# Nine buffers for x, loaded ahead of the tables, and half of the first channel tile's products between the last transposes, in a decoder trunk step

## What is computed

```
xn = rmsnorm(x, norm1_g)
proj = xn @ w_in                 # 1024 -> 2816 columns
conv_out = conv_mixer(proj[..., :1024])      # GLU, causal depthwise conv of width 31, LayerNorm, swish
rwkv_out = rwkv_mixer(proj[..., 1024:])      # RWKV-7 time mixing, 8 heads of 64
h = x + concat(conv_out, rwkv_out) @ w_out
h = h + hier_moe(rmsnorm(h, norm2_g))        # top group of 4, then top 2 of its 8 experts
y = rmsnorm(h, norm_f_g)
```

## Time and profile before

| | |
|---|---|
| median of 3 runs | 1312.06 us (1311.66 to 1314.58) |
| the profiled execution, its own time | 1316.22 us |
| its span | 1314.5 us |
| TensorE busy | 1156.6 us (88%) |
| VectorE, ScalarE, GpSimd busy | 706.1, 326.5, 224.3 us |
| chain that ended last, by engine | TensorE 78%, VectorE 11%, DMA 4% |

### The profile page before, as it was taken

How to read it: one execution, slowest core, us unless ns; L and a number is a source line. 1 busy time by engine, 2 the same in 40 slices (tenths; PEclk the granted TensorE clock), 3 DMA queues, 4 the chain that set the end, 5 groups by cost and what they waited for, 6 DMA issues and landing times.

```text
span 1314.5 us, 23739 instructions
## 1 busy us (share of the span) xinstructions
PE 1156.6 (88%) x9144; PEld 662.7 (50%) x9145; DVE 706.1 (54%) x1252; ACT 326.5 (25%) x616; POOL 224.3 (17%) x278
## 2 busy tenths in 40 slices
PE   4999999999999599999979899984599999999910
PEld 3455555555545588888866455553233333333300
DVE  4278889972224578888852223227243344344346
ACT  4100001111202245555531112111122232322221
POOL 5000000000002212333300001000232333333000
PEclk9799999999998799999987999985699999999965
DMA  6411111110000110111232221127479989999556
GB/s 206 101 32 32 33 32 35 38 38 20 0 0 1 15 17 15 18 19 17 40 87 105 87 74 64 40 83 327 168 282 335 328 317 336 397 408 409 226 220 225
DMA packets 100794, 171.81 MB, mean 131 GB/s; under 512 B 47751, under 2 KB 72190, under 8 KB 91423
## 3 DMA queue, kind: packets, MB, share of 16 engines
q1 hardware_dynamic: 93215, 152.70, 32.9%
q0 software_dynamic: 7488, 17.84, 3.8%
HBM read 153.83 MB, written 26.11 MB: 137 GB/s over the span
## 4 chain that ended last, share of the span: by engine, by line
PE 78%; DVE 11%; DMA 4%; issue 3%; ACT 2%; SPq 1%; POOL 0%; ACTq 0%; POOLq 0%; DVEq 0%
PE ps L1417 26%; PE ps L1847 14%; PE ps L1721 10%; PE ps L1877 7%; PE ps L1444 4%; PE ps L1465 2%; PE ps L1834 2%; DMA arena<-y_rows 2%; DVE arena L2151 1%; PE ps L1749 1%; PE ps L1453 1%; DMA arena<-in_x_prompt_dram 1%; DVE arena L2154 1%; PE ps L1431 1%; PE ps L1661 1%
## 5 line engine op out<-in xcount | busy, mean ns | idle before, releaser
L1417 PE MATMUL ps<-arena 128*128 128x512 f32 (+1 forms) x1056 | 347.6, 491 | 0.6 <-ACT arena L898 0.6
L1417 PEld LDWEIGHTS ps<-arena 128*128 128x128 f32 x1056 | 175.8, 192 | 173.6 <-issue 172.9
L1847 PE MATMUL ps<-arena 128*64 x416 | 192.6, 607 | 7.0 <-DVE arena L2545 6.0
L1850 PE MATMUL ps<-arena 128*64 128x512 f32 x416 | 192.6, 607 | 0.0
L1977 DVE SCALAR_TENSOR_TENSOR arena<-arena,cw 128x1024 f32<-128x1024 f32 x240 | 168.2, 780 | 0.4
L1721 PE MATMUL ps<-arena 128*128 128x512 f32 (+1 forms) x288 | 128.3, 600 | 0.0
L1847 PEld LDWEIGHTS ps<-arena 128*64 128x64 f32 x416 | 55.7, 139 | 118.4 <-issue 118.4
L1444 PE MATMUL ps<-arena 64*64 64x64 f32 x2864 | 98.8, 222 | 13.8 <-DVE arena L2163 9.9
L1444 PEld LDWEIGHTS ps<-arena 64*64 64x64 f32 x2864 | 92.1, 138 | 18.8 <-DVE arena L2163 11.0
L1877 PE MATMUL ps<-arena 128*64 x208 | 96.5, 607 | 2.4 <-ACT arena L1230 2.4
L1880 PE MATMUL ps<-arena 128*64 128x512 f32 x208 | 96.5, 607 | 0.0
(11 more groups left out here) (323 smaller groups left out, 1527.1 us busy)
## 6 DMA issues: line engine op xcount, KB each, us to landing
arena<-in_w_exp_gate_dram SPq DMA_DIRECT2D x32, 1024.0 KB
arena<-in_w_exp_up_dram SPq DMA_DIRECT2D x32, 1024.0 KB
arena<-in_w_exp_down_dram SPq DMA_DIRECT2D x32, 1024.0 KB, 8.7
arena<-in_w_in_dram SPq DMA_DIRECT2D x22, 512.0 KB, 4.0
arena<-in_x_prompt_dram SPq DMA_DIRECT2D x16, 512.0 KB, 6.0
arena<-y_rows SPq DMA_DIRECT2D x8, 1024.0 KB
arena<-in_w_out_dram SPq DMA_DIRECT2D x2, 2048.0 KB, 9.5
xn_rows<-arena SPq DMA_DIRECT2D x8, 512.0 KB, 2.9
```

The source lines that it names most:

```text
L1417: ins = pe.matmul(pr[:, n0:n1], win[q % 6][:, c, :], xnT[:, c, n0:n1], start=(c == 0), stop=(c == DC - 1))
L1847: pe.matmul(banks(b)[0:HS, :], xgT[b][:, c, 0:HS], wring_gu[:, bass.ds(slot, 1), 0:2, c, :].rearrange("p a w f -> p (a w) f"), start=(c == ...
L1850: ins = pe.matmul(banks(b)[HS:P, :], xgT[b][:, c, HS:P], wgu[b][:, :, c, :], start=(c == 0), stop=(c == DC - 1))
```

## The change

`x_in` gets nine places, in the part of the arena that later holds zs, so no load of x waits for a buffer. SyncE issues x0, the gain, x1, x2, x3, the first w_in tile, x4 to x7, the second w_in tile, x8, then the 18 tables, then w_in tiles 2 to 5. Nine semaphores (`x_here`) tell of the tiles; six of them are used later for other ends, whose counts therefore start at 16 (`16 + ...` in those waits). The transposes of x use PSUM banks 4 to 7 instead of 0 to 3. The eight products of the first 512 tokens of q = 0 (blocks c = 0 to 7) are laid behind the transposes of tiles 5, 6, 7 and 8, two each. The tables' transposes come behind them all, into banks 3, 6 and 7, and VectorE unloads them after its last copy. The wait for the unloaded tables stands before q = 1. ScalarE runs one Sqrt on a column of zeros first, which loads its table ahead of the first square.

```diff
-        x_in = [at(O_XR + s * D, D) for s in range(3)]
+        x_in = [at(O_ZS + (1 + s) * D, D) for s in range(NT)]
...
+        x_here = [*x_loaded, s_loaded, fin_stored, *xn2_stored]
...
+        x_here += fin_out
...
             def load_x(i):
-                if i >= 3:
-                    sp.wait_ge(xn_done, i - 2)
                 src = x_prompt[0, i * P:(i + 1) * P, :] if i < NT - 1 else x_sample.rearrange("b t d -> (b t) d")
-                sp.dma_start(x_in[i % 3][0:rows_of(i), :], src).then_inc(x_loaded[i % 3], 16)
+                sp.dma_start(x_in[i][0:rows_of(i), :], src).then_inc(x_here[i], 16)
...
             load_x(0)
             sp.dma_start(gain[:, :], norm1_g[0, :].partition_broadcast(P)).then_inc(gain1_in, 16)
-            load_x(1)
-            load_x(2)
+            for i in range(1, NT):
+                load_x(i)
+                if i in (3, 7):
+                    load_w_in(i // 7)
...
-            for i in range(3, NT):
-                load_x(i)
...
+            act.wait_ge(iota_done, 1)
+            act.activation(stat[:, 7, 0:1], stat[:, 7, 0:1], ACT.Sqrt)
             square(0)
...
             def tables():
                 pe.wait_ge(tables_in, 16 * N_TABLES)
-                tb = banks(6)
+                pe.wait_ge(xT_act, NT - 1)
+                pe.wait_ge(xT_dve, NT - 1)
+                tb = banks(3)
...
                 for c in range(DC):
-                    ins = pe.transpose(banks(2 * (i % 2) + c // 4)[:, (c % 4) * P:(c % 4) * P + r],
+                    ins = pe.transpose(banks(4 + 2 * (i % 2) + c // 4)[:, (c % 4) * P:(c % 4) * P + r],
                                        xn[i % 2][0:r, c * P:(c + 1) * P], ident[0:r, 0:r])
                 ins.then_inc(xT_psum, 1)
-                if i == 3:
-                    tables()
-
+                if i == 5:
+                    pe.wait_ge(w_loaded[0], 16)
+                if i >= 5:
+                    for c in range(2 * i - 10, 2 * i - 8):
+                        pe.matmul(banks(0), win[0][:, c, :], xnT[:, c, 0:512], start=(c == 0), stop=(c == DC - 1))
+            tables()
             pe.wait_ge(xT_act, NT)
             pe.wait_ge(xT_dve, NT)
-            pe.wait_ge(tables_done, 1)
-            pe.wait_ge(const_ready, 2)
...
             for q in range(MT):
                 pe.wait_ge(w_loaded[q % 6], 16 * (q // 6 + 1))
+                if q == 1:
+                    pe.wait_ge(tables_done, 1)
+                    pe.wait_ge(const_ready, 2)
...
-                for n0 in range(0, N, 512):
+                for n0 in range(0 if q else 512, N, 512):
...
-                if i == 5:
+                if i == NT - 1:
+                    copy_T(i)
                     dve.wait_ge(tables_psum, 1)
-                    tb = banks(6)
+                    tb = banks(3)
```

More of the change, by code:

```diff
@@ L434, in hybrid_decoder_step @@
         wd_in = [w_loaded[5], *x_loaded]
-        wd_0 = [16 * len(range(5, MT, 6))] + [32 * (NT // 3)] * 3
+        wd_0 = [16 * len(range(5, MT, 6))] + [16 + 16 * (NT // 3)] * 3
         gu_here, wd_here, gu_copied, down_copied = (sem(n) for n in ("gu_here", "wd_here", "gu_copied", "down_copied"))
@@ L466, in load_x, with load_w_in @@
             def load_x(i):
-                if i >= 3:
-                    sp.wait_ge(xn_done, i - 2)
                 src = x_prompt[0, i * P:(i + 1) * P, :] if i < NT - 1 else x_sample.rearrange("b t d -> (b t) d")
-                sp.dma_start(x_in[i % 3][0:rows_of(i), :], src).then_inc(x_loaded[i % 3], 16)
+                sp.dma_start(x_in[i][0:rows_of(i), :], src).then_inc(x_here[i], 16)
+            def load_w_in(q):
+                t = ORDER[q]
+                sp.dma_start(win[q % 6][:, :, :], w_in[0, :, t * P:(t + 1) * P].rearrange("(c p) n -> p c n", p=P))\
+                    .then_inc(w_loaded[q % 6], 16)
             load_x(0)
             sp.dma_start(gain[:, :], norm1_g[0, :].partition_broadcast(P)).then_inc(gain1_in, 16)
-            load_x(1)
-            load_x(2)
+            for i in range(1, NT):
+                load_x(i)
+                if i in (3, 7):
+                    load_w_in(i // 7)
             for vec, name in ((mu_shift, "mu"), (k_k, "k_k"), (k_a, "k_a"), (r_k, "r_k"), (a0, "a0"), (gn_g, "gn_g"),
@@ L500, in store_tail @@
                         .then_inc(tables_in if k == 1 else tails_out, 16)
-            for q, t in enumerate(ORDER):
+            for q in range(2, MT):
                 if q >= 6:
                     sp.wait_ge(proj_done, q - 5)
-                sp.dma_start(win[q % 6][:, :, :], w_in[0, :, t * P:(t + 1) * P].rearrange("(c p) n -> p c n", p=P))\
-                    .then_inc(w_loaded[q % 6], 16)
+                load_w_in(q)
                 if q in (16, 17, 20, 21):
@@ L578, in _ @@
                 if i == 5:
-                    sp.wait_ge(fin_stored, 32 * (CT + 1))
+                    sp.wait_ge(fin_stored, 16 + 32 * (CT + 1))
                 load_residual(i)
@@ L621, in _ @@
                 if e == RW - 1:
-                    sp.wait_ge(xn2_stored[0], 16 * ((NT + 1) // 2))
-                    sp.wait_ge(xn2_stored[1], 16 * (NT // 2))
+                    sp.wait_ge(xn2_stored[0], 16 + 16 * ((NT + 1) // 2))
+                    sp.wait_ge(xn2_stored[1], 16 + 16 * (NT // 2))
                 load_gate_up(e, e)
@@ L670, in _ @@
                 result_out(i)
-            sp.wait_ge(fin_out[0], 16 * ((NT + 1) // 2))
-            sp.wait_ge(fin_out[1], 16 * (NT // 2))
-            sp.wait_ge(fin_stored, 32 * (CT + 1))
+            sp.wait_ge(fin_out[0], 16 + 16 * ((NT + 1) // 2))
+            sp.wait_ge(fin_out[1], 16 + 16 * (NT // 2))
+            sp.wait_ge(fin_stored, 16 + 32 * (CT + 1))
             sp.wait_ge(tails_out, 16 * 13)
@@ L830, in _ @@
             ins.then_inc(iota_done, 1)
-            pool.wait_ge(xn2_stored[0], 16 * ((NT + 1) // 2))
-            pool.wait_ge(xn2_stored[1], 16 * (NT // 2))
+            pool.wait_ge(xn2_stored[0], 16 + 16 * ((NT + 1) // 2))
+            pool.wait_ge(xn2_stored[1], 16 + 16 * (NT // 2))
             pool.wait_ge(lg_done, NT)
@@ L885, in square @@
                 r = rows_of(i)
-                act.wait_ge(x_loaded[i % 3], 16 * (i // 3 + 1))
-                act.activation(squares[0:r, :], x_in[i % 3][0:r, :], ACT.Square,
+                act.wait_ge(x_here[i], 16)
+                act.activation(squares[0:r, :], x_in[i][0:r, :], ACT.Square,
                                accum_out=stat[0:r, 0, i:i + 1]).then_inc(sq_done, 1)
@@ L1897, in link @@
                 dve.wait_ge(dve_chain, step[0])
-            dve.memset(stat[:, 7, :], 0.0)
+            dve.memset(stat[:, 7, :], 0.0).then_inc(iota_done, 1)
             dve.memset(hx[:, :, 0:HB], 0.0)
@@ L2411, in _ @@
             dve.wait_ge(lg_done, NT)
-            dve.wait_ge(iota_done, 1)
+            dve.wait_ge(iota_done, 2)
             gl, el = lg[:, :, 0:NG], lg[:, :, NG:]
```

19 lines of the change are left out of this document (9 added, 10 removed).

## The result

| | before | changed |
|---|---|---|
| median (7 runs each) | 1311.66 us | 1301.24 us |
| lowest to highest | 1306.09 to 1314.58 | 1296.66 to 1306.75 |
| ratio, 95% interval | | 0.9924 [0.9897, 0.9951] |
| the profiled execution | 1316.22 us | 1301.24 us |
| ScalarE gets the first channel tile | 59.75 us | 46.91 us |

What follows compares the result with a forecast made beforehand. TensorE alone was taken to bound the projections, with idle holes in the first 41 us; hand-over at 48.7 instead of 59.75 saves 11.1 us, so median 1312.06 becomes 1301.0 us, range about 1298.0 to 1306.5.

Steps and rivals of the forecast that it cites:

- Loads: Transfers of x before the tables: at 307 or 257 GB/s, x4 lands at 14.0 to 16.3, x8 at 21.6 to 25.5.
- the rival of a late x: x4 to x8 land 1 to 4 us late, delaying tile 5; gain 7 to 10 us, about 1304; chance 0.15.
- Their window, 26 to 31: Transfers of the tables, 1.4 MB issued after x, end at 26 to 31 us, before TensorE needs them.
- Pace: Loop of copy, square, mean, scale, transposes: 5.24 us for two tiles, so tile 5's transposes start at 23.3.
- Clock: TensorE rises from half to full clock between 26.6 and 29.4 us, taken as 28.0, after gapless work.
- Walk: TensorE's work from tile 5 to the first channel tile's hand-over, ending at 48.7 instead of 59.75, 11.1 us earlier.
- the 0.6 for joins: Waits at eight joins in TensorE's work from tile 5 on, at most 0.56 us each, 0.6 us in all.
- The tables' term: TensorE's transposes of the tables behind tile 8: 3.0 us, from 3.91 at half clock less 0.9.
- Costs nothing: VectorE's 3 us of table unloading hides under the 8.8 us second half; the hidden Sqrt table load gives 0.
- The rest: Behind the hand-over nothing changes, so the gain reaches the end; rival of no change, 1312 us, chance 0.04.
- Clock stays down: Mixed work on TensorE never raises the clock: hand-over 66.3, whole time 1318.6 us; later rise costs half per us; chance 0.03.

Runs made afterwards that it cites:

- tables_at_tile3: The changed kernel with the tables' transposes back behind tile 3 and their unloading back in VectorE's iteration 5; hand-over 55.47 us, whole time 1311.24 us (one run).
- squares_ahead: The changed kernel with ScalarE squaring tile i+3 ahead of its copy of tile i; hand-over 44.24 us, ratio 0.9912 to the kernel before the change.
- second_half_twice: The changed kernel with the second half of q = 0 computed twice; hand-over 53.52 us, median 1309.86 us, ratio 0.998 to the kernel before the change.
- no_sqrt_first: The changed kernel without the Sqrt ahead of the first square; hand-over 46.62 us, ratio 0.9935 to the kernel before the change.
- warm_up: The changed kernel with 50 identity transposes on TensorE before tile 0; hand-over 46.12 us, ratio 0.9904 to the kernel before the change.

## Why the prediction was right

The forecast was 1301.0 us, the median is 1301.24. That closeness is luck: my walk was 1.8 us too long (12.84 gained at the hand-over, not 11.1), while the median fell by only 10.4, and the two misses hide each other within the spread of the runs. The mechanism came as forecast. By its steps:

- *Loads.* All squares found their tile, also x4, so the rival of a late x did not come. The rates of the earlier trace rows were too low for x, though: they average over a stretch with the gain and one with the tables' small rows. The kernel before has 422 GB/s from 6 to 8 us, and the changed one 422 and 418 from 12 to 16, where x4 to x7 move. By the bytes moved in issue order (an estimate from the view by stretch), x4 was in at about 12.5 and x8 at about 19, not at 14.0 to 16.3 and 21.6 to 25.5. So the trace comes near the rate that the prediction took from the Trainium skill (DMA: Bandwidth & Descriptors, Anatomy of one DMA); that section gives its formula for DMAs that GpSimd issues, and these are issued by SyncE. What I missed is that SyncE is held behind a w_in tile: the tables left at 13.94 instead of about 6.5, at the 0.45 us that most issues took. Why it is held, no run tested. It cost nothing, since TensorE asks for the tables at 35.82 and they landed by about 28 (the row at 28.19 in tables_at_tile3). Their window, 26 to 31, held, but from a later start and higher rates than I had reckoned with.
- *Pace.* Tile 5 at 23.3, measured 23.36; the squares at 13.26 and 15.21 against 13.3 and 15.2. Tile 4 came at 20.43 and not at 21.3: tile 2's transposes ran at full clock, so ScalarE copied it at 17.16 instead of 18.0, and the loop passed that on. The experiment squares_ahead confirms that the square was in the loop.
- *Clock.* I took a rise at 28.0 out of 26.6 to 29.4; it came at 27.4, and that is partly luck. The reasoning had two flaws. In the old run TensorE had worked without a gap since 22.8, where tile 3's transposes began, and not since 24.69, so the rise came some 7 us behind and not 5.3. And the changed kernel's clock wasn't low throughout: it was full for tile 2 and fell at 17.2. Other kernels with the same work up to there rose at 21.7 (second_half_twice) and 26.7 (no_sqrt_first). From the start of gapless work to the rise these traces show 1.3 to some 7 us, so that time forecasts nothing; my range was too narrow on the early side, and the hand-over moves by 2 us with it.
- *Walk.* Measured from tile 5 on: products behind tile 5 to 27.99 (I had 28.4), tile 8's transposes 0.63 (0.9), tables 2.3 (3.0), and the 0.6 for joins was not needed, because the next tile's first weights load while the last pass still runs. The second half took 8.8 as summed (38.10 to 46.91). Hand-over 46.91 instead of 48.7. The tables' term was the one most off: at full clock the fourteen small transposes also went faster (0.94 us of weight loads against 1.56 before), where I had kept them as they were.
- *Costs nothing.* The Sqrt: confirmed. VectorE's unloading now starts at 38.30 and ends before 42, under the second half: confirmed.
- *The rest.* One to one to the end of the projection (350.1 and 350.1), and by the nine kernels together to the end of the kernel, with a slope of 0.96.
- *Clock stays down* did not come, but its price per us was right: the products behind tile 5 ran some 2.3 us at half clock (25.12 to 27.4) and took 3.03 us, 1.15 more than the 1.88 at full clock.

## What to carry to other kernels

More buffers for an input give nothing while other transfers stand before it in the issuing queue and other work before it on the engines; look at which engine holds each tile, and move the side work (here the tables) behind all tiles on every queue at once. Where an engine waits in small gaps for a slower loop, lay work of the next stage there only from the tile on at which its operands are complete, and check that its weights are loaded by then. When the loop itself can be named as a sum of rows (copy, square, mean, scale, transpose), the cheapest next gain is to take one member out of it.

## What the runs showed of the hardware

The granted clock column says 1.00 from the start of a trace, but the weight loads of 223 to 230 ns at the first tiles in every kernel that does not warm up, against eight in 0.85 us together at tile 0 of warm_up, show half clock until a first rise. Durations are the better witness there.

With transposes of 1.09 us in a beat of some 2.1 us the clock did not hold (warm_up, tiles 2 to 3); with six more transposes in every pause (0.82 us for six) and the squares further ahead it did, in both kernels that tried.

The same code takes different times with the clock's luck. From hand-over to the last projection product the twelve profiles show 350.1 (six of them), 351.7 to 351.8 (five) or 353.4 us (one). TensorE is busy there all the time, and the granted clock says why. Summed over stretches of 2 us, the length times what the clock lacks to 1.00 comes to 1.7 us in each of the first six, 3.4 in the five and 5.1 in the one; less that, all twelve took 348.3 to 348.4 us. In second_half_twice, the one, that is why the end of the projection is 9.9 us later than in the change and the hand-over only 6.6.

The recurrence (last projection product to first output product) takes 296.5 to 302.8 us: the changed kernel 298.4 and no_sqrt_first 302.8, though no instruction of it differs. By the view by stretch, with TensorE alone:

```profile
398.40:701.20 302.80, 266.34 (x5616) 0.92 0.16 36
```

```profile
392.20:688.70 296.50, 260.50 (x5616) 0.94 0.16 37
```

The shorter one has the higher clock (0.94 against 0.92) and less busy time for the same 5616 records. By the same sum the clock lacks 18.8 us in the three profiles of 296.5 to 296.6 us and 23.9 in the six of 302.3 to 302.8; the three between (297.9 to 299.2) lack 20.5 to 22.2 and don't line up as well. The 6 us between these profiles of an unchanged stage go a good way towards the 10 us between the lowest and the highest run of one kernel. That the clock is the whole cause there is argued from these rows and not tested. It is also why single parts of this change had to be read at the hand-over and not from the whole time.
